# Softmax reciprocals in their own unit, ahead of weight splits, and four reorderings in a two-block transformer kernel on Trainium2

## The reference

```python
p = jax.nn.softmax(s, axis=-1).astype(v.dtype)
return jnp.einsum('bhqk,bkhd->bqhd', p, v)
```

## Time and profile before

| | us |
|---|---|
| median of 3 runs | 3266.33 (3265.73 to 3266.57) |
| profiled execution | 3266.29 |
| its span on the core | 3264.7 |
| TensorE busy | 3226.8 (99%) |
| VectorE busy | 1815.4 (56%) |
| ScalarE busy | 1304.5 (40%) |
| GpSimd busy | 573.9 (18%) |

### The profile page before, as it was taken

How to read it: one execution, slowest core, us unless ns; L and a number is a source line. 1 busy time by engine, 2 the same in 40 slices (tenths; PEclk the granted TensorE clock), 3 DMA queues, 4 the chain that set the end, 5 groups by cost and what they waited for, 6 DMA issues and landing times.

```text
span 3264.7 us, 38209 instructions
## 1 busy us (share of the span) xinstructions
PE 3226.8 (99%) x15436; PEld 2687.1 (82%) x15436; DVE 1815.4 (56%) x2740; ACT 1304.5 (40%) x1989; POOL 573.9 (18%) x492
## 2 busy tenths in 40 slices
PE   9999999999999999999999999999999999999998
PEld 7878888888887888888888888888888898788887
DVE  6865675444438655855444455554544268974433
ACT  5643553333227533633232333332423248843221
POOL 1420131111003210320110022110211013531101
PEclk9999999999999999999999999999999999999999
DMA  3122223232321222232323322222232323223322
GB/s 136 33 72 84 96 93 103 94 109 91 99 97 52 66 72 81 100 97 97 98 96 100 103 81 81 88 84 91 91 104 90 103 78 97 97 83 101 101 97 84
DMA packets 85136, 295.60 MB, mean 91 GB/s; under 512 B 9568, under 2 KB 12128, under 8 KB 84960
## 3 DMA queue, kind: packets, MB, share of 16 engines
q1 hardware_dynamic: 84384, 292.76, 27.2%
q10 hardware_dynamic: 576, 0.40, 0.0%
HBM read 291.02 MB, written 2.10 MB: 90 GB/s over the span
## 4 chain that ended last, share of the span: by engine, by line
PE 84%; DVE 9%; ACT 2%; POOL 2%; issue 2%; DMA 1%; SPq 0%; DVEq 0%; ACTq 0%; POOLq 0%
PE bank L313 82%; PE bank L316 2%; DVE wl L563 2%; DMA raw<-in_wts 1%; POOL u_g L585 1%; DVE c_kl L563 1%; ACT wh L533 1%; DVE small L1293 1%; DVE m_ptl L563 0%; DVE u_uc L559 0%; POOL b_p L588 0%; DVE b_qk L553 0%; DVE u_t L559 0%; POOL m_ql L585 0%; DVE m_yf L553 0%
## 5 line engine op out<-in xcount | busy, mean ns | idle before, releaser
L563 DVE TENSOR_TENSOR wl<-raw,wh 128x1024 fp32r<-128x1024 f32 (+1 forms) x531 | 665.7, 1256 | 776.3 <-ACT wh L533 775.3
L313 PE MATMUL bank<-zh,wh 128*128 128x512 f32 (+1 forms) x2652 | 1024.7, 386 | 5.5 <-ACT zh L533 5.4
L313 PE MATMUL bank<-zl,wh 128*128 128x512 f32 (+1 forms) x2652 | 1018.4, 384 | 3.1 <-DVE zl L566 2.9
L313 PE MATMUL bank<-zh,wl 128*128 128x512 f32 (+1 forms) x2652 | 1018.9, 384 | 0.9 <-DVE wl L563 0.9
L533 ACT ACTIVATE wh<-raw 128x1024 fp32r<-128x1024 f32 (+1 forms) x531 | 556.1, 1052 | 525.4 <-PE bank L313 465.1
L313 PEld LDWEIGHTS bank<-zh,wl 128*128 128x128 f32 x2652 | 498.6, 188 | 104.1 <-DVE wl L563 3.9
L313 PEld LDWEIGHTS bank<-zh,wh 128*128 128x128 f32 x2652 | 498.9, 188 | 102.0 <-ACT zh L533 6.0
L313 PEld LDWEIGHTS bank<-zl,wh 128*128 128x128 f32 x2652 | 498.8, 188 | 100.2 <-DVE zl L566 5.5
L313 PE MATMUL bank<-f_mh,wh 128*128 128x512 f32 (+1 forms) x748 | 285.1, 381 | 0.0
L313 PE MATMUL bank<-f_mh,wl 128*128 128x512 f32 (+1 forms) x748 | 283.3, 379 | 0.0
L313 PE MATMUL bank<-f_ml,wh 128*128 128x512 f32 (+1 forms) x748 | 280.7, 375 | 0.0
(11 more groups left out here) (337 smaller groups left out, 4427.1 us busy)
## 6 DMA issues: line engine op xcount, KB each, us to landing
raw<-in_wts SPq DMA_DIRECT2D x529, 512.0 KB, 3.3
c_nb<-in_c_bias SPq DMA_DIRECT2D x16, 384.0 KB, 3.2
x<-in_xT SPq DMA_DIRECT2D x8, 256.0 KB, 5.9
out<-x SPq DMA_DIRECT2D x13, 128.0 KB, 1.8
b_mask<-in_b_mask SPq DMA_DIRECT2D x2, 576.0 KB, 4.5
r_d<-in_decay SPq DMA_DIRECT2D x4, 256.0 KB, 2.7
raw<-in_wts SPq DMA_DIRECT2D x2, 256.0 KB, 3.4
m_t<-in_mla_tab SPq DMA_DIRECT2D x2, 256.0 KB, 4.7
```

The source lines that it names most:

```text
L313: return self.e.matmul(out, l, r, start=start, stop=stop, skip_group_check=inside)
L563: return self.e.tensor_tensor(out, src, b32(hi), ALU.subtract)
```

## The change

- `Dve` gets a `lag`. While `vector_div` waits for an exponential, VectorE needs to have split only the chunks up to two (`RAWS`) behind those that ScalarE had split, not all of them. The demand stays on record and is met at the next wait.
- Latent and neighbourhood attention: reciprocal and scaling of a block move to the block's own unit or iteration, on VectorE behind the low half of the transposed block (in neighbourhood attention behind y, gates and projections too) and ahead of the weight splits, which move back with them there.
- Dilated attention: on ScalarE the exponential goes first in iterations 3, 5 and 7, and the weight copy goes to the end of every iteration; on VectorE the reciprocals of iterations 0, 3, 5 and 7 go ahead of the transposed low half.
- The last pair of y of latent attention is split in iteration 2 of the first dilated part, on ScalarE and GpSimd.
- The keys' low halves of head 3 in neighbourhood attention are written one iteration later than those of head 2.
- In the first loop the weight chunks to be split before tile i go from i // 2 (0, 0, 1, 1, 2, 2, 3, 3) to (3i + 2) // 8 (0, 0, 1, 1, 1, 2, 2, 2).

```diff
@@ -549,6 +549,12 @@
 
 
 class Dve(Splitter):
+    lag = 0
+
+    def weights(self, upto, least=-1):
+
+        super().weights(upto, least - self.lag)
+
     def tt(self, out, a, b, op):
         return self.e.tensor_tensor(out, a, b, op)
 
@@ -694,7 +700,7 @@
     L.weights(0)
     L.wait_ge("cst0", "g")
     for i in range(8):
-        L.weights(i // 2)
+        L.weights((3 * i + 2) // 8)
         L.wait_ge(f"xi{i}", "x")
         scalar_x(L, ("mix", 0), i, g)
         if i == 0:
@@ -1127,7 +1133,9 @@
 
 def vector_div(L, i, *key):
     m, c = L.m, i % 8
+    L.lag = RAWS
     L.wait_ge("ex", *key, i)
+    L.lag = 0
     L.e.reciprocal(m.rd[:, c:c + 1], m.den[:, c:c + 1]).then_inc(*L.tell("rc", *key, i))
 
 
@@ -1277,7 +1285,7 @@
             scalar_k_even(L, l, i // 8 + 1)
         if i % 8 == 0 and 0 < i < 32:
             scalar_k_odd(L, l, i // 8)
-        if i >= 16 and i % 8 == 0:
+        if 16 <= i < 40 and i % 8 == 0:
             scalar_y(L, m.m_yf, m.ya[0], (i - 16) // 8, (i - 16) // 8, "mla", l)
     L.ahead()
 
@@ -1291,8 +1299,6 @@
             c = i % 8
             L.wait_ge("qk", "mla", l, i)
             L.e.tensor_reduce(m.mn[:, c:c + 1], m.bank[4 + i % 2], AX.X, ALU.min).then_inc(*L.tell("mn", "mla", l, i))
-        if 1 <= i < 33:
-            vector_div(L, i - 1, "mla", l)
         if i < 4:
             vector_mv(L, l, (0, 3, 1, 2)[i])
         if i >= 9 and i % 4 == 1:
@@ -1303,6 +1309,8 @@
             hi, lo = [f4(x)[:, :, 128 * (j % 2):128 * (j % 2) + 128] for x in m.m_pt[hb % 2]]
             L.wait_ge("hi", "pt", "mla", l, j)
             L.lo(lo, f4(m.bank[turn_bank(j)]), hi).then_inc(*L.tell("lo", "pt", "mla", l, j))
+        if i < 32:
+            vector_div(L, i, "mla", l)
         L.ahead_of(level)
         if i % 4 == 1 and i < 29:
             vector_q_turn(L, l, i // 4 + 1)
@@ -1319,11 +1327,11 @@
 def gpsimd_mla(L, l):
     m = L.m
     for i in range(41):
-        if 1 <= i < 33:
-            gpsimd_div(L, i - 1, m.m_p[(i - 1) % 4], "mla", l)
-        if i % 4 == 2 and i < 30:
+        if i < 32:
+            gpsimd_div(L, i, m.m_p[i % 4], "mla", l)
+        if i % 4 == 1 and i < 29:
             gpsimd_q(L, l, i // 4 + 1)
-        if i >= 16 and i % 8 == 0:
+        if 16 <= i < 40 and i % 8 == 0:
             gpsimd_y(L, m.m_yf, *m.ya, (i - 16) // 8, (i - 16) // 8, "mla", l)
 
 
@@ -1572,6 +1580,10 @@
     for i in range(13):
         for n in () if p else at(p, i, 1):
             scalar_b(L, ("b", l, 1) + n)
+        first = i % 2 and 3 <= i < 8
+        if first:
+            L.wait_ge("mn", *key, i, 1)
+            scalar_exp(L, i, m.b_p[i % 2], m.b_p[i % 2], *key)
         if 1 <= i < 9:
             j = i - 1
             r = j % 4
@@ -1582,12 +1594,13 @@
                 *L.tell("hi", "pt", *key, j))
             L.wait_ge("tp", *key, j, 2)
             L.cp(m.b_pt12[j % 2], m.bank[3][:, 0:256]).then_inc(*L.tell("hi", "pt12", *key, j))
-        L.ahead()
-        if i < 8:
+        if i < 8 and not first:
             L.wait_ge("mn", *key, i, 1)
             scalar_exp(L, i, m.b_p[i % 2], m.b_p[i % 2], *key)
         if i == p == 0:
             scalar_bv(L, l, 1, range(2, 4))
+        if p == 0 and i == 2:
+            scalar_y(L, m.m_yf, m.ya[0], 3, 3, "mla", l)
         for n in at(p, i, 1) if p else ():
             if n[0] == "g":
                 scalar_gate(L, l, 0, n[1])
@@ -1595,7 +1608,7 @@
             scalar_y_move(L, m.b_yt, i // 9, *key)
         if i == 10:
             scalar_y(L, m.b_yf, m.yb[0], 0, p, *key)
-    L.ahead()
+        L.ahead()
 
 
 def vector_dil(L, l, p):
@@ -1653,17 +1666,18 @@
                 vector_gate(L, l, 0, n)
             elif ("g", n) not in new:
                 vector_proj(L, l, 0, n)
-        if i == 0:
-            vector_div(L, 0, *key)
-            if p == 0:
-                vector_bv(L, l, 1, range(2, 4))
+        early = i < 8 and (i == 0 or i % 2 and i > 1)
+        if early:
+            vector_div(L, i, *key)
+        if i == p == 0:
+            vector_bv(L, l, 1, range(2, 4))
         if 1 <= i < 9:
             j = i - 1
             r = j % 4
             hi, lo = [f4(x)[:, :, 128 * (r % 2):128 * (r % 2) + 128] for x in m.b_pt]
             L.wait_ge("hi", "pt", *key, j)
             L.lo(lo, f4(m.bank[6]), hi).then_inc(*L.tell("lo", "pt", *key, j))
-        if 0 < i < 8:
+        if i < 8 and not early:
             vector_div(L, i, *key)
         L.ahead_of(level)
         for x, n in new:
@@ -1687,6 +1701,8 @@
         if i < 8:
             gpsimd_div(L, i, L.m.b_p[i % 2], *key)
         if p == 0:
+            if i == 2:
+                gpsimd_y(L, L.m.m_yf, *L.m.ya, 3, 3, "mla", l)
             for n in at(p, i, 2):
                 gpsimd_b(L, ("b", l, 1) + n)
 
@@ -1905,10 +1921,6 @@
                     L.wait_ge("tp", *key, (i - 6) // 2)
                 L.min_sum(m.c_p[i % 6], m.bank[4 + i % 2][:, 0:256], m.c_nb[h % 2][:, 256 * var:256 * var + 256], BIG,
                           m.mn[:, cc:cc + 1]).then_inc(*L.tell("mn", *key, i))
-        if 1 <= it < 17:
-            for i in (2 * it - 2, 2 * it - 1):
-                vector_div(L, i, *key)
-        L.ahead_of(level)
         if it >= 5 and it % 2 and it < 20:
             vector_y_add(L, m.b_yt, m.b_yf, (it - 5) // 2, *key, view=GRID, oview=TOKENS)
         if 2 <= it < 18:
@@ -1921,6 +1933,10 @@
                 (vector_c_q if x == "q" else vector_c_k)(L, l, n)
             else:
                 (vector_gate if x == "g" else vector_proj)(L, l, 1, n)
+        if it < 16:
+            for i in (2 * it, 2 * it + 1):
+                vector_div(L, i, *key)
+        L.ahead_of(level)
         if it >= 8 and it % 4 == 0:
             vector_y(L, m.b_yf, *m.yc, (it - 8) // 4, (it - 8) // 4, *key)
         for x, n in at_n(it, 2):
@@ -1930,9 +1946,8 @@
                 vector_c_k_lo(L, l, 2 * n)
         if it == 1:
             vector_c_q_lo(L, l, 1)
-        if it == 2:
-            vector_c_k_lo(L, l, 2)
-            vector_c_k_lo(L, l, 3)
+        if it in (2, 3):
+            vector_c_k_lo(L, l, it)
         for x, n in at_n(it, 3):
             if x == "k":
                 vector_c_k_lo(L, l, 2 * n + 1)
```

## The result

The kernel after takes 3261.24 us (median of 20 runs, 3259.95 to 3263.59) against 3266.3 (20 runs, 3264.46 to 3268.31): ratio 0.9984, 95% interval 0.9977 to 0.9991. That is 5 us less, where 9 were forecast.

What follows compares the result with a forecast made beforehand. TensorE bounds the kernel, busy 3226.8 of 3264.7 us; VectorE could become the bound in latent attention. Terms: start -1.5, latent -0.8, dilated -5.5, neighbourhood -1.2, sum -9.0; 3266.3 - 9.0 = 3257.3 us, range 3249 to 3268.

Steps and rivals of the forecast that it cites:

- the prediction's own mark for faster: Whole kernel: below 3259.8 us counts as faster, since a measurement can tell about 0.2%, 6.5 us; chance 0.57.
- Rival 1: All named stalls go, with VectorE keeping pace in the latent part: 3243 us, halfway 3250; chance 0.15.
- rival 2: Latent attention: waiting for the exponential makes VectorE's pace 2 to 4 us slower a layer, 3262 to 3266; chance with another 0.21.
- signs of being wrong: Latent stage shorter by over 3 us or longer, or scalings of 1.5 us and more ahead of waiting transposes.
- the step that failed: Latent attention: VectorE needs 6.6 us more, has 7.6 usable idle; TensorE's gain taken as -0.4 us a layer.
- 7 + 3.5: Latent attention, VectorE's added waits: 7 us in about 20 plain units, 3.5 us where a weight copy precedes the exponential.
- 3.9: Latent attention, VectorE time coming back: 2.7 us from seven shorter weight splits, some 1.2 us at ten rotations.
- Begin of the dilated part: Moving the last latent y's split gives -1.4 and -0.5 us; after block 0's late scaling, -0.5 and 0 remain.
- The block of the scaling: Block 0 of the dilated part: GpSimd's scaling, held by a VectorE split, ends about 0.9 us later than it could.
- First dilated part: Earlier exponentials and reciprocals remove TensorE waits, including 1.17 us at the last block: -2.5 us a layer.
- Neighbourhood attention: Stall of 0.79 + 0.27 us at 391.64 goes, new wait of 0.5 to 0.8 near 383: net -0.6 a layer.
- The start: First loop: writing token tile 4 before weight chunk 2's split removes TensorE's wait, -1.5 us.

Runs made afterwards that it cites:

- the two experiments: Kernel before with only head 3's key low halves one iteration later: 3265.20 us; kernel before with only the neighbourhood order, without that move: 3265.48 us.
- the one with the exponential first: Kernel after with ScalarE taking the exponential ahead of the weight copy in latent attention: 3260.48 us, ratio 0.9981.

## Why the prediction was right and where it was off

- **The sum.** 3257.3 was forecast and 3261.2 measured, inside the range. It is not below 3259.8, the prediction's own mark for faster: by that mark it fell on "the same", which had a chance of 0.35 where faster had 0.57, and the ratio of 0.9984 (to 0.9991) says only that the change gains a little. Rival 1 isn't it. In the latent part the mechanism of rival 2 is what happened, at 1.8 us a layer instead of its 2 to 4. Part of the closeness is luck: in the two profiles the latent part is 4.4 us worse than its term, and the neighbourhood part, for a reason that had no term, 2.5 better than its own. Two of the prediction's signs of being wrong came true: the latent stage got longer, and a scaling of 1.80 us stood ahead of waiting transposes (181.21).
- **Latent attention: the step that failed** is "has 89.0 - 78.4 = 10.6 of idle time, of which I count 7.6 as usable". VectorE's new work was no more than forecast: waits of 8.2 us for 7 + 3.5 (4.1 in 25 plain units, 4.2 in the 6 with a split right behind), and 1.7 less busy for 3.9. That is 6.5 us more, for a forecast of 6.6. But only what VectorE waits for TensorE can be filled, and between the first and the last minimum that is 4.8 us of 9.4 (7.9 less 3.1 ahead of the first minimum); the rest waits for yal, for the keys' high halves and for splits. 6.6 less 4.8 would have given +1.8, which is what came. The sum by the rows: +8.3 at the reciprocal, -4.8 for scores, -0.6 at the splits, +0.7 for yal, -0.1 others = +3.5 idle, less 1.7 busy = +1.8.
- **What the working did not see:** the wait had a filling at hand. The lag was priced as a wait that the change adds; that a split of 1.2 us would fit into it was known from the earlier trace rows, and the order without lag was not worked out. It is worth 2.5 us a layer in the latent part. In the run without it the waits of plain units stay (4.2), and those of the units with a split are gone.
- **Begin of the dilated part.** The block of the scaling was forecast by the earlier trace rows and came so (1.80 for 0.91). TensorE's stand at 174.46 fell from 1.13 to 0.24 us, as forecast, and its new wait of 1.0 at block 0 ate it: 0.0 in layer 0, where 0.5 were forecast. The stand at 174.46 differs between profiles of unchanged code (0.51 to 1.40), and the five profiles with these edits and the collision at block 0 give from -0.8 to +0.1 here, so the 0.5 can't be called wrong. The Trainium skill's rule (SBUF — State Buffer, "Who interferes with whom": a shared port pair between VectorE and GpSimd, an exclusive lock) agrees with both directions here: the splits became short (1207 ns for 1605), the scalings long (1004 ns for 722).
- **First dilated part.** -2.7 and -2.6 for -2.5: the wait of 1.17 us at the last block went, nothing late stood behind it.
- **The second dilated part** gives back 0.6 and 0.5 us that the prediction had at 0 because the part had no stall; it priced later splits only in the first part, and took them to be hidden there. Here one is not. It ended at 285.90 us in the kernel before, 6 us ahead of its matmul at 291.94; in the kernel after it stands behind the next minimum and ends at 290.11, and the matmul waits for it, as the timeline of after shows:

```profile
288.89 1.22 DVE L569 TENSOR_TENSOR wl<-raw,wh 128x1024 fp32r<-128x1024 f32 x1
...
290.16 0.50 PE L313 MATMUL bank<-zh,wl 128*128 128x512 f32 x1 [0.28 <-DVE wl L569]
```

Every profile with the dilated edits gives back 0.5 to 0.6 us here, with the lag or without it, and those without these edits nothing. Which of the dilated edits moves the split was not tried.
- **Neighbourhood attention.** The stall went nearly as forecast (0.9 us for 1.06), and the wait for the split near 383 cost 0.15, not 0.5 to 0.8: the chunk's first matmul came 0.27 us behind the one ahead of it and the next 0.33 behind that, for 0.23 each. Another 1.0 and 1.2 us in the two layers came later in the part and had no term; by the two experiments it needs both edits. (The 1.65 us named for the two moved keys' halves don't follow from the row of 4.34: the two that stayed take 1.81, so 2.5 went. The sum doesn't use it.)
- **The start.** The term was right in size: 1.6 us for 1.5 in the stretch of the stall, in all nine profiles with the edit. That the table shows 1.3 is the beginning of the profiles, which differ: at 14.30 us the matmuls already lie 0.1 to 1.9 us behind the ones of before.

## What to carry to other kernels

Where an engine comes to wait for a short-lived result, put the work that is ready ahead of the wait, not behind it, as long as it fits into the wait (work that doesn't fit was not tried): here splits of 1.2 us ahead of the reciprocals were worth 8 us in all, 5 in latent attention and 2 at block 0 of the dilated part, where they kept GpSimd's scaling clear. Of an engine's idle time in a stretch count as usable only what it waits for the bound engine; idle time that ended on a third engine stayed here. Work that lies well ahead of its user before a reordering need not lie so behind it: follow each one. A stall that moves from one engine's queue to another's shows in the busy time of the second (GpSimd +50 us with the same instructions).

## What the runs showed of the hardware

- A scaling on GpSimd that began 0.18 us behind a VectorE subtraction took 2.10 us at 82.99 for 0.69, as if it stood through that split and most of the VectorE instruction right behind (83.93 to 84.61). With no such second instruction it took 1.6 (1.80 for the 768-column one, for 0.91). In the kernel after, 12 of the 64 scalings of latent attention take 1.58 to 2.11 us; in the one with the exponential first, none more than 1.06.
- In the profile of the keys' low halves alone TensorE's granted clock fell to half for some 3.4 us. Windows (us; busy PE, PEld, DVE, ACT, POOL; clock, DMA share, GB/s) and timeline:

```profile
176.00:184.00 8.00, 8.00 (x35) 6.57 (x36) 4.87 (x12) 4.03 (x10) 0.91 (x1) 0.79 0.19 66
178.00:180.00 2.00, 2.00 (x7) 1.52 (x6) 1.85 (x5) 0.87 (x2) 0.00 (x0) 0.50 0.00 0
```

```profile
175.19 0.47 PE L313 MATMUL bank<-b_k,b_q 128*128 128x512 f32 x1 [1.40 <-ACT b_k L533]
...
177.37 0.63 PE L313 MATMUL bank<-zl,wh 128*128 128x512 f32 x1
177.80 0.63 PE L313 MATMUL bank<-zh,wl 128*128 128x512 f32 x1
```

From 177.37 to 180.36 the matmuls come 0.43 us apart instead of 0.23, at the lower of the two levels (1.2 GHz, where 2.4 is full). It began some 2 us behind a stand of 1.40 us at 175.19; the execution lost 1.3 us there. In the kernel before a stand of 1.13 us at the same matmul left the clock at 1.00, and so did stands of 1.02 and 1.03 us there in two other profiles. What decides between the two was not tried.
- At the start of all profiles the matmuls come 0.43 us apart for a while, though the granted clock of the stretch reads 1.00; how long (to 8.6 us in before, to 12.4 where the start alone was changed) differs.
